# Two directions of a chunked recurrence on banks and order of their own, and three stages around it joined or pipelined

## The reference

```python
px = modulate(rmsnorm(x, norm1_g[l]), sh1, sc1) @ w_in[l]      # also for 256 context tokens
# for both directions d, over 256 context and 1024 x tokens, 8 heads of 64x64 state:
def step(s, inp):
    r_t, w_t, k_t, v_t, a_t, b_t = inp
    sa = jnp.einsum('bhvk,bhk->bhv', s, a_t)
    s = s * w_t[:, :, None, :] + sa[..., :, None] * b_t[:, :, None, :] + v_t[..., :, None] * k_t[:, :, None, :]
    return s, jnp.einsum('bhvk,bhk->bhv', s, r_t)
...
x = x + g1 * (jnp.concatenate([a_x, b_x], axis=-1) @ w_out[l])
hx = modulate(rmsnorm(x, norm2_g[l]), sh2, sc2)
x = x + g2 * expert_choice_ffn(hx, router_w[l], ...)            # softmax scores, top-k per expert, 16 experts
return rmsnorm(x, final_g)
```

## Time and profile before

| what | value |
|---|---|
| median of 3 runs | 3004.51 us (3002.74 to 3013.65) |
| the profiled execution | 3004.86 us, span 3003.1 us |
| busy PE, DVE, ACT, POOL | 2475.9, 1637.8, 989.9, 633.9 us |
| recurrence | about 1563 to 2065 us |
| out projection | about 2129 to 2244 us |
| routing until the scores are there | 2244 to 2313 us |
| final norm | about 2969 to 3003 us |

### The profile page before, as it was taken

The page is one execution under the profiler, slowest core; times in us unless marked ns, Lnnn a source line. Parts: engine busy times, 40 slices in busy tenths (PEclk is TensorE's granted clock), DMA queues, the critical chain, the costliest instruction groups (busy, mean ns, idle before and its releaser), DMA issues. The chain is left out here.

```text
span 3003.1 us, 56691 instructions
## 1 busy us (share of the span) xinstructions
PE 2475.9 (82%) x23638; PEld 1885.2 (63%) x23638; DVE 1637.8 (55%) x2058; ACT 989.9 (33%) x1552; POOL 633.9 (21%) x618
## 2 busy tenths in 40 slices
PE   4698997959998469999858878888676299999993
PEld 1487654537676458887326767775465188888882
DVE  2793447721114332466455555553424899999993
ACT  2121442220103230000334333333102177777772
POOL 0221347302110013221034444440000010100000
PEclk8799999979999769999559999997695599999996
DMA  9232003421103211110141011101435199999993
GB/s 381 70 137 76 21 1 114 119 102 35 52 21 136 100 56 57 64 36 22 67 133 30 19 25 25 31 12 42 173 109 188 44 408 407 388 394 399 398 380 133
DMA packets 132727, 405.61 MB, mean 135 GB/s; under 512 B 55090, under 2 KB 64946, under 8 KB 102690
## 3 DMA queue, kind: packets, MB, share of 16 engines
q1 hardware_dynamic: 119268, 359.53, 31.9%
q0 software_dynamic: 4608, 16.78, 2.3%
q10 hardware_dynamic: 8640, 26.19, 2.2%
HBM read 346.85 MB, written 55.61 MB: 134 GB/s over the span
## 5 line engine op out<-in xcount | busy, mean ns | idle before, releaser
L3070 DVE TENSOR_TENSOR ex_wl<-ew_raw,ex_wh 128x2048 fp32r<-128x2048 f32 x192 | 435.5, 2289 | 42.5 <-ACT ex_wh L3032 39.0
L3032 ACT ACTIVATE ex_wh<-ew_raw 128x2048 fp32r<-128x2048 f32 x192 | 367.5, 1919 | 110.0 <-PE ex_U L2976 40.3
L125 PE MATMUL sp_acc<-b2h_hi,sp_wh 128*128 128x512 f32 (+1 forms) x528 | 194.9, 369 | 11.8 <-POOL sp_wl L1614 11.8
L125 PE MATMUL sp_acc<-b2h_lo,sp_wh 128*128 128x512 f32 (+1 forms) x528 | 194.6, 369 | 0.0
L125 PE MATMUL sp_acc<-b2h_hi,sp_wl 128*128 128x512 f32 (+1 forms) x528 | 194.5, 368 | 0.0
L2162 ACT ACTIVATE rc_xt<-rc_ps 128x256 f32<-128x256 f32 x200 | 67.7, 389 | 192.1 <-PE rc_ps L2331 191.6
L2953 POOL DMA_INDIRECT x<-ex_o,ex_at x16 | 26.5, 1656 | 494.1 <-DVE ex_o L3093 494.1
L1100 DVE TENSOR_TENSOR merge_sg<-b_pj,merge_sg 128x512 f32<-128x512 f32 x16 | 11.1, 693 | 218.2 <-ACT merge_sg L1086 218.2
L2229 DVE TENSOR_TENSOR rc_x<-rc_x,rc_ps 128x256 f32<-128x256 f32 x160 | 60.1, 417 | 120.7 <-PE rc_ps L2317 120.5
L125 PE MATMUL merge_acc<-merge_hh,merge_wh 128*128 128x512 f32 x256 | 101.5, 397 | 26.4 <-POOL merge_wl L119 21.1
L1612 POOL CAST sp_wh<-sp_w 128x1024 fp32r<-128x1024 f32 x26 | 27.1, 1042 | 434.2 <-DMA sp_w<-in_w_conv 250.2
(11 more groups left out here) (471 smaller groups left out, 6278.9 us busy)
## 6 DMA issues: line engine op xcount, KB each, us to landing
ew_raw<-in_exp_gate SPq DMA_DIRECT2D x64, 1024.0 KB, 8.1
ew_raw<-in_exp_up SPq DMA_DIRECT2D x64, 1024.0 KB, 9.4
ew_raw<-in_exp_down SPq DMA_DIRECT2D x64, 1024.0 KB, 8.1
b_pj<-in_ada_w SPq DMA_DIRECT2D x24, 1024.0 KB, 18.9
rc_ac<-ac SPq DMA_DIRECT2D x40, 256.0 KB, 4.1
merge_w<-in_w_merge SPq DMA_DIRECT2D x16, 512.0 KB
ac<-rp_ac SPq DMA_DIRECT2D x4, 2048.0 KB, 7.1
pr_w<-in_w_main SPq DMA_DIRECT2D x14, 512.0 KB
```

What stands on the lines that cost most here:

```text
L125: ins = nc.tensor.matmul(out, w[a][:, k, :], h[b][:, k, cols], start=(first and n == 0), stop=(last and n == 2))
L3032: nc.scalar.activation(wh[:, n % RING], raw[:, n % RING], ACT.Copy).then_inc(q["w_hi"], 1)
L3070: V.tensor_tensor(wl[:, n % RING], raw[:, n % RING], wh[:, n % RING].bitcast(f32), ALU.subtract).then_inc(q["w_lo"], 1)
```

## The change

Four edits.

1. In the recurrence PSUM is cut anew: a pair of banks `chain0` and `chain1` for each direction's level work, one bank `turned`, one bank `own_half` for all work within a half, one pair `crossing`. `t1_done`, `xp_done` and `low_done` count per direction. PE runs direction 0's products, the transposes of both, then direction 1's products, and so on. The right side's two halves are added on DVE (new) in place of two ACT copies and a second term of 16 matmuls in `solved`. The scaling of the state moves from DVE to the end of GpSimd's body. The places of keys, solved, outputs, row turns, state and the next chunk's `lower` all change on PE, DVE and ACT.
2. The loads of constants and of the affine rows, and the affine columns themselves, move into `mixer_norms`; the phases ahead of it go. The 22 tables are issued on SP between block 5's and block 6's load.
3. `out_scored` takes the place of `out_norm` for the second block and of the first half of `route`: the norm, the store of h, the transposes and the scores of block b run among the matmuls of blocks b+1 and b+2. The two 2 MB loads are cut in halves.
4. `final_norm` takes mean, root and reciprocal block by block and has 8 y buffers.

```diff
 def rwkv_chunks(...)
+        joint = {n: ph.sem(n) for n in ("xt_done", "xi_done", "pk_done", "g_crossed", "g_done", "u_done", "y_done", "y_crossed", "s_done",
+                                        "brows_done", "rows_done", "v_done")}
+        X = [ph.ps(f"chain{d}", [P, 2, 512]) for d in range(2)]
+        Z, V_, W = ph.ps("turned", [P, 512]), ph.ps("own_half", [P, 512]), ph.ps("crossing", [P, 2, 512])
...
             def _(pool):                       # end of body
+                    if old is not None:
+                        for d in range(2):
+                            b, s = t[d], q[d]
+                            pool.wait_ge(s["summed"], i)
...
+                            G.tensor_tensor(b["S"][:], b["sum"][:], b["e_end"][:, 1 - sl].to_broadcast([P, HP, CK]), ALU.mult).then_inc(s["state"], 1)
...
             def _(dve):
-                        dve.wait_ge(joint["t1_done"], LEVELS * i + l + 1)
+                        dve.wait_ge(s["t1_done"], LEVELS * i + l + 1)
...
                 def body(i, sl, half, old, here, following):
                     masked(i, 0)
                     advanced(i, 0, sl)
                     masked(i, 1)
+                    if old is not None:
+                        right_side(i)
                     advanced(i, 1, sl)
+                    factor(i, sl, 0)
                     masked(i, 2)
+                    factor(i, sl, 1)
                     advanced(i, 2, sl)
                     if old == "all":
-                        outputs(i - 1)
+                        outputs(i - 1, 0)
                     masked(i, 3)
+                    advanced(i, 3, sl)
+                    if old == "all":
+                        outputs(i - 1, 1)
+                    masked(i, 4)
                     if old is not None:
                         summed(i)
                     if following is not None:
                         first(i + 1, 1 - sl)
+                        lower(i + 1, 1 - sl)
...
             def _(pe):
+                def chain(d, a, w, l, r):
+                    for j, s, c in product(range(HP // 2), range(2), range(2)):
+                        f = c ^ s ^ d
+                        k, h, at = slice(f * CK, (f + 1) * CK), 2 * j + c, a + j * w
+                        last = M(X[d][c * CK:(c + 1) * CK, f, at:at + w], l[k, h], r[k, h], start=True, stop=True)
+                    return last
...
+                def level(i, l, sl):
+                    def products(d):
...
+                            pe.wait_ge(s["x_next"], (LEVELS - 1) * i + l)
+                        chain(d, 0, CK, b["lm"][:, sl, :, 0:CK], b["x"][:, sl]).then_inc(s["t1_done"], 1)
+                    products(0)
...
+                        last = turned(part(Z, d), t[d]["x"][:, sl])
+                    last.then_inc(joint["xt_done"], 1)
+                    products(1)
...
                 def body(i, sl, old, following):
+                    level(i, 0, sl)
                     if old is not None:
                         right_side(i, 1 - sl)
                         right_side_of_state(i, 1 - sl)
                     advanced(i, 0, sl)
+                    level(i, 1, sl)
+                    keys(i, sl, old)
+                    advanced(i, 1, sl)
+                    if old == "all":
+                        outputs_of_state(i, 1 - sl)
+                    level(i, 2, sl)
+                    advanced(i, 2, sl)
                     if old is not None:
+                        each("lk_ready", i + 1)
                         solved(i, 1 - sl)
+                    level(i, 3, sl)
                     if old == "all":
                         outputs(i, 1 - sl)
+                        each("y_added", 2 * (i - CTX_CK))
...
+                    rows("bst", i, sl, "brows_done")
+                    advanced(i, 3, sl)
+                    each("b_rows", i + 1)
+                    rows("kst", i, sl, "rows_done")
+                    level(i, 4, sl)
                     if old is not None:
+                        state(i, 1 - sl, old)
                     if following:
                         lower(i + 1, 1 - sl)
+                    inverted(i, sl)
+                    each("k_rows", i + 1)
+                    each("v_staged", i + 1)
...
+                    last.then_inc(joint["v_done"], 1)
 def mixer_norms(...)
+                for dst, src in ((rows[:], mod_rows), (n1[:], n1_row)):
+                    sp.dma_start(dst, src).then_inc(q["rows_loaded"], 16)
                 for b in range(N):
+                    if b == 6:
+                        for dst, src in constants:
+                            sp.dma_start(dst, src).then_inc(q["constants_loaded"], 16)
+def out_scored(...)                            # PE
+                    for k in range(KD):
...
+                        if k == 2 and b >= 2:
+                            scored(b - 2)
+                        if k == 6 and b >= 1:
+                            turned(b - 1)
+                        for h in range(2):
...                                            # DVE, ahead of its loop
+                dve.wait_ge(q["rows_loaded"], 80)
+                V.scalar_tensor_tensor(a_row[:], a_row[:], 1.0, xn[:, 0, :], ALU.add, ALU.mult).then_inc(q["a_made"], 1)
 def final_norm(...)                            # DVE
+                mean(0)
                 for b in range(NB):
+                    if b + 1 < NB:
+                        mean(b + 1)
+                    dve.wait_ge(q["rooted"], b + 1)
+                    V.reciprocal(st[:, 3, b:b + 1], st[:, 2, b:b + 1]).then_inc(q["inverted"], 1)
...
+                    V.scalar_tensor_tensor(y[:, b, :], x[:, b, :], st[:, 3, b:b + 1], row[:], ALU.mult, ALU.mult).then_inc(q["ready"], 1)
```

More of the change, by code:

```diff
@@ L1437, with mixer_norms @@
 DECAY = 0.6065306597126334
[L1440 to L1462 removed]
+def mixer_norms(nc, T, blocks, parts, mod_rows, n1_row, ab, constants):
     N = len(blocks)
@@ L1552, in _ @@
             def _(pe):
+                pe.wait_ge(q["rows_loaded"], 32)
+                for k in range(2 * KD):
+                    last = nc.tensor.transpose(pc[:, k, :], rows[:, k * P:(k + 1) * P], T.ident[0:2, 0:2])
+                last.then_inc(q["rows_turned"], 1)
                 for b in range(N):
@@ new lines, in right_side_of_state, with keys, solved @@
+                def right_side_of_state(count, sl):
+                    each("state", count)
+                    staying(V_, lambda b: b["ar"][:, sl, :, 0:CK], lambda b: b["S"]).then_inc(joint["g_done"], 1)
+                def keys(i, sl, old):
+                    each("stk", i + 1)
+                    if old is not None:
+                        each("g_copied", i)
+                    crossing(2 * CK, (lambda b: b["kst"][:, sl], lambda b: b["ar"][:, sl])).then_inc(joint["pk_done"], 1)
+                def solved(count, sl):
+                    each("g_ready", count)
+                    each("inverse", count)
+                    crossing(CK, (lambda b: b["xt"][:, sl], lambda b: b["g"])).then_inc(joint["u_done"], 1)
@@ new lines, in outputs, with outputs_of_state, rows @@
+                def outputs(count, sl):
+                    each("u_ready", count)
+                    crossing(CK, (lambda b: b["u"], lambda b: b["lm"][:, sl, :, CK:]), (lambda b: b["v"], lambda b: b["lk"][:, sl, :, CK:])).then_inc(joint["y_crossed"], 1)
+                def outputs_of_state(count, sl):
+                    each("g_ready", count)
+                    staying(V_, lambda b: b["S"], lambda b: b["ar"][:, sl, :, CK:]).then_inc(joint["y_done"], 1)
+                def rows(name, i, sl, done):
+                    for d in range(2):
+                        last = turned(part(V_, d), t[d][name][:, sl])
+                    last.then_inc(joint[done], 1)
@@ L2408, in body, with state @@
+                def state(i, sl, old):
+                    each("u_ready", i)
+                    each("b_rows", i)
+                    each("k_rows", i)
+                    if old == "all":
+                        each("y_added", 2 * (i - CTX_CK) + 1)
+                    crossing(CK, (lambda b: b["brows"][:, sl], lambda b: b["u"]), (lambda b: b["krows"][:, sl], lambda b: b["v"])).then_inc(joint["s_done"], 1)
                 def body(i, sl, old, following):
-                    products(i, 0, sl)
@@ L2414, in body @@
                     advanced(i, 0, sl)
-                    for d in range(2):
-                        pe.wait_ge(q[d]["stk"], i + 1)
-                    crossing(3, 2 * CK, (lambda b: b["kst"][:, sl], lambda b: b["ar"][:, sl])).then_inc(joint["pk_done"], 1)
-                    x_turned(i, 1, sl)
-                    products(i, 1, sl)
+                    level(i, 1, sl)
+                    keys(i, sl, old)
+                    advanced(i, 1, sl)
+                    if old == "all":
+                        outputs_of_state(i, 1 - sl)
```

634 lines of the change are left out of this document (328 added, 306 removed).

## The result

The changed kernel takes 2916.91 us, median of 4 runs (2913.55 to 2920.09), beside 3006.4 us of the kernel before: ratio 0.9699, 95% interval 0.9677 to 0.9722, 3.0% faster. The forecast was 2921 us. The profiled execution took 2913.55 us.

What follows compares the result with a forecast made beforehand. It saw a PE stream with gaps in the recurrence, a PE-bound projection able to hide another stage, and that exposed routing. Gains 21 + 16.6 + 39.5 + 7 = 84 us off 3004.86 gave 2921 us, range 2870 to 2955.

Steps and rivals of the forecast that it cites:

- The idle on issue: Recurrence: PE idles 43.9 us on instruction issue, 2.2 us a chunk, expected near 44 us again.
- The recurrence: New order of the 20 chunks: period near 23.4 us instead of 24.4, gain 21 us.
- the time line: Recurrence chunk placed by operation durations: 21.3 us new, 22.0 old, PE working 18.3; order alone gives 0.7.
- DVE's wait before the subtractions well under 120: Recurrence sign: DVE's wait for PE there, 120.5 us in the kernel before, should fall clearly.
- State on GpSimd: Recurrence: moving the state's scaling to GpSimd puts nothing on the path and gains nothing.
- Constants and affine: Second norms: first square starts earlier, table loads hidden between blocks 5 and 6; gain 16.6 us.
- Projection and scores: Out projection: norm, transposes and scores hidden among later blocks' matmuls; gain 39.5 us, bounds 30 and 46.
- Final norm: Last stage: block-by-block roots let scalings start earlier, 1.8 us each; gain 7.0 us, bounds 4 and 10.
- A: Rival: recurrence's issue idle vanishes into the waits, gain there 61 us, total 2881; chance 0.13.
- B: Rival: recurrence gains nothing because PE's instruction supply binds it, total 2942; chance 0.19.
- C: Rival: bare round trips through `own_half` make the recurrence 28 us a chunk, total 3014; chance 0.03.
- D: Rival: scores not hidden, PE's transposes wait for DVE each block, projection gain 25 us, total 2935; chance 0.07.

Runs made afterwards that it cites:

- after: The changed kernel with all four edits, against the kernel before: 2916.9 us, ratio 0.9699.
- old_recurrence: Changed kernel with the recurrence of the kernel before, all other edits kept: 2935.8 us, ratio 0.9761 to the kernel before.
- early_transposes: Changed kernel with the projection's transposes of the previous block ahead of the third of 8 matmul groups instead of the seventh: 2952.4 us.
- constants_first: Changed kernel with the 22 table loads issued ahead of the first norm block's load, not between blocks 5 and 6: 2926.9 us.
- joint_products: Changed kernel with the products of both directions ahead of the transposes, semaphores still per direction: 2897.7 us.
- fewer_waits: Changed kernel without PE's recurrence waits on counts already waited for (34 a chunk), staggered products kept: 2888.4 us.
- joint_fewer_waits: joint_products without PE's recurrence waits on counts already waited for (34 of 94 a chunk): 2885.4 us.
- solved_twice: Changed kernel with the 16 matmuls of `solved` issued twice, same values and no new wait: 2937.4 us.
- old_fewer_waits: old_recurrence without PE's recurrence waits on counts already waited for: 2916.5 us.
- state_on_dve: Changed kernel with the state's scaling moved from GpSimd back to DVE, behind the sum: 2913.4 us.

## Why the prediction was right

**The idle on issue.** Most of it goes with the fetch of instructions. In the trace of after, PE pauses 39 times for more than 0.7 us within 19 periods, 41.7 us in all (31 of them, 35.1 us, on issue), and 30 of these pauses, 31.7 us, end 1.2 to 1.5 us after an instruction block of 16 KB has landed. Only 5% of all PE's matmuls start in that stretch behind a landing. In before it is 25 of 39. Blocks come every 4.2 us on the median and never closer than 3.4. That the fetch is the cause is argued from this timing; no run changes the fetch alone.

The prediction kept this idle nearly whole; 2.5 us a chunk became 2.3. Its 43.9 us (2.2 a chunk) was only the largest of three such rows of before; in the 19 periods they add up to 48.3, so that 43.4 came out "near 44" is a coincidence of the accounting. The Trainium skill ("Runtime: NRT & Kernel Launch", "Instruction fetch mechanics") has it that crossing a block's boundary is mostly hidden. By number this trace agrees, for 72 of the 102 blocks bring no pause over 0.7 us; by cost it doesn't, for the other 30 bring 31.7 of 446.6 us. Why those 30 and not the others isn't shown.

**The recurrence.** Forecast 21 us and a period of 23.4; measured 18.9 (old_recurrence) and 23.5. The number came out, its working did not, so that it came this close is luck. The step that failed is the time line. It had PE at 18.3 us of work a chunk where the trace has 19.7, for it counted half a group at half the time of a group (0.28, where the trace has 0.37 to 0.39 for the first half), and a wait that is satisfied at nothing. And it is the line of a chunk with outputs, set beside the mean over all chunks. The starts of the masked copy part the two kinds. The first five periods are bodies without outputs:

| us | first five periods | each of the other 14 | of the 19, at granted clock 0.50 |
|---|---|---|---|
| before | 115.2 | 24.85 | 32.7 |
| old_recurrence | 112.8 | 25.26 | 27.9 |
| after | 103.7 | 24.44 | 12.6 |
| early_transposes (recurrence of after) | 102.0 | 24.26 | 1.8 |
| constants_first (recurrence of after) | 102.8 | 24.58 | 11.8 |
| joint_products | 99.4 | 23.64 | 11.7 |
| fewer_waits | 100.0 | 23.27 | 1.9 |
| joint_fewer_waits | 104.8 | 22.92 | 13.5 |
| solved_twice | 106.7 | 25.69 | 15.9 |
| old_fewer_waits | 109.6 | 23.78 | 17.5 |

So a chunk with outputs takes 24.4 us, not the 23.5 of the line and the kept idle. It gains 0.4 us over before (0.8 over old_recurrence), and 11.5 of the 17 us gained in these periods (9.1 of 21) come from the first five, of which the prediction says nothing. The clock is a rival that no run parts from the order: before spends 20 us more at 0.50 than after, and after itself 11 us more than early_transposes, whose 19 periods are 4.2 us shorter with the same recurrence.

The gain was put together as 0.7 us of order and the rest of issue and dependencies. The runs price other parts: 16 matmuls in `solved` put back are worth 1.07 us a chunk (solved_twice), to which the prediction gave the words "4% fewer instructions" and in its time line at most PE's 0.5 us (1.05 less 0.56); the stagger, which it priced at 1.2 us a level in place of a joint round trip, costs 0.8 us a chunk (joint_products). If these add up, the banks, the places of the fillers and the rest make up for that, 24.57 - 22.68 - 1.07 = 0.8. The last is a remainder and was not measured by itself, and the same recurrence gives periods of 23.28 to 23.56 in three traces, so each part is good to some 0.3.

The sign "DVE's wait before the subtractions well under 120" came too, 66.3 us, but says little: with the wait before the masks it only fell from 164.9 to 156.6.

**State on GpSimd.** Forecast nothing, measured nothing clear of noise (state_on_dve).

**Constants and affine.** Forecast 16.6, measured 16.8 between landmarks; the hiding place is right too (constants_first: 10.0 for 10.8).

**Projection and scores.** Forecast 39.5, measured 41.8 between landmarks. The added PE time is 93.5 - 7 x 10.88 = 17.3 us (forecast 17.7). From the gate of the last block to the reduce it takes 14.6, forecast 15.9: behind the scores stand 1.25 us (2228.52 to 2229.77), not 2.4. The forecast wait of 1.5 us in block 1 isn't there.

**Final norm.** Forecast 7.0, measured 8.4: scalings come 1.45 us apart, not 1.8.

**Rivals.** A (idle on issue vanishes) fell with the 43.4 us left and the period of 23.5. B (no gain, since the stream is bound) is right in part: 16 matmuls cost nearly twice their PE time (solved_twice), and the change itself takes such instructions out, which B missed. But joint_products, the same instructions in another order, gains 16 to 19 us, and that no bound on instructions alone explains. C and D did not come: the only bare round trip of `own_half` is the copy of the rows, 4.8 us of PE's waits in 19 periods, and PE waits for a normalised block only behind the last gate (5.40 us), where the prediction had it.

## What to carry to other kernels

Where PE runs many small matmuls from straight code, count instructions, not only microseconds: 16 matmuls of 64x64 (64 instructions) cost 1.07 us a chunk for 0.58 us of PE time. First leave out waits whose count the engine has already waited for: in three orders of this recurrence that gave 12 to 28 us by the medians, in the old order as much as the whole rewrite. Don't judge a time line of one kind of chunk by a mean over several kinds. And when work is hidden in another engine's stream, place it later than it is ready: a wait of 2.7 us cost 4.3 to 5.6.

## What was not expected of the hardware

A semaphore increment alone in PE's stream takes 0.15 us of it, and 64 of them a chunk cost 192 us in the whole program. Groups of 384 matmul records of 64x32 took as long as those of 64x64 (8.0 and 8.3 us). The granted clock fell to 0.68 on the mean for 4.4 us behind an idle stretch of 2.7 us. What stays open is how a satisfied wait costs PE busy time as well as idle time (a part can be the clock: PE spends 12.6 us of the 19 periods at 0.50 in after and 1.9 in fewer_waits), and why the stagger costs 0.8 us a chunk with outputs while the repeated waits are there and 0.35 without them.
